# A two-tile transformer kernel: choosing the first tile's experts in lots beside the second tile's projection, with the index woven into the first

## What is computed

```python
qa, ka, va, iq, ik, iw, qb, kb, vb = split(h @ w_in)       # 2760 columns
score = einsum(relu(iq . ik), iw)                          # index: keeps the best 64 keys of each query
out_a = softmax attention of qa over the kept ka, va;  out_b = block attention of qb, kb, vb
x = x + concat(out_a, out_b) @ w_out
h = rms_norm(x)                                            # the expert layer
q = (h @ w_q).reshape(t, 8, 2, 128)                        # 8 heads, two halves
v_half, i_half = top_k(q . sub_keys, 16)                   # 128 keys a half
top_s, pos = top_k(all sums of the two halves' values, 16) # 16 experts of 16384 a head
w = softmax(top_s) * gelu(u_tab[expert] . h)
x = x + sum over 128 experts of w * v_tab[expert]
```

## Time and profile before

| what | value |
|---|---|
| median of three runs | 2173.9 us (2172.73 to 2174.57) |
| profiled execution | 2178.61 us, its span 2176.9 us |
| PE busy | 1676.0 us (77%) |
| DVE busy | 1487.9 us (68%) |
| ACT busy | 797.0 us (37%) |
| POOL busy | 649.8 us (30%) |
| moved by DMA | 747.39 MB, of it 536.90 MB by gathers; mean 343 GB/s |
| mean granted PE clock | 0.891 of full speed |

### The profile page before, as it was taken

How to read it: one execution, slowest core, us unless ns; L and a number is a source line. 1 busy time by engine, 2 the same in 40 slices (tenths; PEclk the granted TensorE clock), 3 DMA queues, 4 the chain that set the end, 5 groups by cost and what they waited for, 6 DMA issues and landing times.

```text
span 2176.9 us, 20643 instructions
## 1 busy us (share of the span) xinstructions
PE 1676.0 (77%) x6478; PEld 1014.4 (47%) x6478; DVE 1487.9 (68%) x3088; ACT 797.0 (37%) x2066; POOL 649.8 (30%) x524
## 2 busy tenths in 40 slices
PE   8688777847776865877777577665777899898998
PEld 4473333713323444332344433544333465668986
DVE  3359776798766679966666896758777464565644
ACT  1212462224324422432452234212545343444542
POOL 0003444444433443543243354435444000000000
PEclk9699988879999886999889799877889999999999
DMA  7248999999999999999999999999999775474552
GB/s 283 97 164 332 421 391 416 415 405 422 410 421 415 400 420 404 405 419 421 401 372 422 388 386 421 421 421 421 387 402 395 296 275 190 174 278 156 176 192 97
DMA packets 105947, 747.39 MB, mean 343 GB/s; under 512 B 12912, under 2 KB 13552, under 8 KB 16752
## 3 DMA queue, kind: packets, MB, share of 16 engines
q0 software_dynamic: 73728, 536.90, 60.3%
q1 hardware_dynamic: 31536, 207.08, 24.7%
q10 hardware_dynamic: 576, 2.10, 0.3%
HBM read 744.98 MB, written 1.05 MB: 343 GB/s over the span
## 4 chain that ended last, share of the span: by engine, by line
PE 41%; DMA 21%; DVE 20%; ACT 10%; issue 6%; DVEq 1%; PEldq 0%; POOL 0%; ACTq 0%; PEld 0%; SPq 0%; POOLq 0%
DMA sb_work<-in_peer_uv,sb_expert 17%; PE ps_acc L1453 11%; PE bank L492 6%; DVE sb_work L1417 5%; PE bank L1246 4%; DVE sb_x L1425 4%; PE bank L1939 2%; DMA sb_wring<-in_peer_w_q 2%; PE bank L559 2%; PE ps_acc L559 2%; ACT L1433 2%; PE ps_acc L561 2%; PE ps_acc L560 2%; PE bank L560 2%; PE bank L561 2%
## 5 line engine op out<-in xcount | busy, mean ns | idle before, releaser
L2497 POOL DMA_INDIRECT sb_work<-in_peer_uv,sb_expert x512 | 645.6, 1261 | 1033.5 <-PE ps_acc L1453 466.5
L1453 PE MATMUL ps_acc<-sb_work,sb_diag 128*128 128x512 f32 x1304 | 688.3, 675 | 314.2 <-ACT sb_diag L1442 267.9
L1417 DVE CUSTOM_DVE_ANT_0 sb_work<-sb_work,sb_h 128x1024 f32<-128x1024 f32 x512 | 619.9, 1223 | 190.4 <-DMA sb_work<-in_peer_uv,sb_expert 180.5
L1453 PEld LDWEIGHTS ps_acc<-sb_work,sb_diag 128*128 128x128 f32 x1304 | 264.7, 215 | 680.9 <-issue 672.0
L1433 ACT ACTIVATE sb_dots<-sb_dots 128x1 f32<-128x1 f32 x512 | 102.2, 200 | 527.6 <-DVE sb_dots L1417 492.6
L1425 DVE SCALAR_TENSOR_TENSOR sb_x<-sb_work,sb_weight,sb_x 128x1024 f32<-128x1024 f32 x186 | 238.5, 1282 | 81.1 <-ACT sb_weight L1434 81.1
L553 DVE TENSOR_TENSOR sb_work_r<-sb_wring,sb_work_r 128x2048 fp32r<-128x2048 f32 (+1 forms) x76 | 138.2, 1840 | 121.4 <-ACT sb_work_r L546 121.4
L546 ACT CAST sb_work_r<-sb_wring 128x2048 fp32r<-128x2048 f32 (+1 forms) x76 | 115.3, 1546 | 115.9 <-PE ps_acc L561 44.1
L1434 ACT ACTIVATE sb_weight<-sb_dots,sb_share 128x1 f32<-128x1 f32 x512 | 150.8, 294 | 16.6
L1246 PE MATMUL bank<-sb_hT,sb_wring 128*128 128x128 f32 x1024 | 125.8, 288 | 21.4 <-DMA sb_wring<-in_peer_w_q 19.3
L1246 PEld LDWEIGHTS bank<-sb_hT,sb_wring 128*128 128x128 f32 x1024 | 123.9, 204 | 24.8 <-issue 23.7
(11 more groups left out here) (326 smaller groups left out, 2154.3 us busy)
## 6 DMA issues: line engine op xcount, KB each, us to landing
sb_wring<-in_w_mix SPq DMA_DIRECT2D x36, 1024.0 KB
sb_wring<-in_peer_w_q SPq DMA_DIRECT2D x32, 1024.0 KB
sb_wring<-in_w_gate SPq DMA_DIRECT2D x32, 1024.0 KB
sb_wring<-in_w_up SPq DMA_DIRECT2D x16, 1024.0 KB
sb_wring<-in_w_down SPq DMA_DIRECT2D x16, 1024.0 KB
sb_wring<-in_mla_w_uq SPq DMA_DIRECT2D x12, 768.0 KB
sb_work<-in_hyb_w_in SPq DMA_DIRECT2D x8, 1024.0 KB, 15.0
sb_wring<-in_hyb_w_out SPq DMA_DIRECT2D x8, 1024.0 KB
```

What stands on the lines that cost most here:

```text
L1417: e.tensor_tensor_reduce(u, u, h[:, t, :], 1.0, 0.0, ALU.mult, ALU.add, dots[:, i:i + 1]).then_inc(dot_ready, 1)
L1453: last = e.matmul(ps_acc[:, b * 512:(b + 1) * 512], diag[:, number % DIAGS, :], ring[:, n % RING, D + b * 512:D + (b + 1) * 512], start=k ...
L2497: pool.indirect_dma_start(ring[:, n % RING, :], None, a["peer_uv"], bass.IndirectOffsetOnAxis(ap=expert[:, t, n % P:n % P + 1], axis=0)).t ...
```

## The change

- **First projection.** The blocks of the input projection come in the order 1, 2, 0, 3, 4, 5, in both tiles. In tile 0 the turn of the rotated heads and the index are woven into the projection's stage (`first_projection`), at fixed places between PE's half blocks; relu has two buffers.
- **open_experts** replaces `route(0, 0)` with `enter_hybrid`. The first 512 query columns and their scores come first, then tile 1's projection; the other three blocks of queries stand behind its blocks 3, 4 and 5 in the order. DVE chooses experts in four lots of two heads, each with its own `experts_ready` and its own shares. The first feed is opened at the beginning of this stage, with six points "early" (3.5 each, adds on DVE) behind lot 0 and 18 points (0.85 each, adds on PE) in each of the lots 1 to 3. ACT waits for a lot's shares before its first pick.
- The turned h of tile 1 is scaled by DVE in two instructions instead of by ACT in eight.
- **Keys** have a tile of their own, 8 KB a partition, and are loaded once a layer; SP's wait for the three engines is gone for layer 0 and is one for PE in layer 1.

`top16`, `select` and the parts of the shares are moved out of `route` and otherwise unchanged; `route` calls them for all heads at once. `index_parts` is the old `index` taken apart. Core of the diff:

```diff
-        def project_parts(xT, w, chunks, cols, empty, engine, tiles, first=None, keeps=0):
+        def project_parts(xT, w, chunks, cols, empty, engine, tiles, keeps=0, order=None,
+                          planned=None, pointed=True):
 
             per, wide = blocking(chunks)
             plan = []
             block = blocks_of(w, chunks, cols, per, wide)
-            for n0 in range(0, cols, wide):
+            for i, b in enumerate(order or range(-(-cols // wide))):
+                if planned:
+                    planned(i)
+                n0 = b * wide
                 wn = min(wide, cols - n0)
                 slots = []
                 for k in range(0, chunks, per):
-                    r = n0 // wide * (chunks // per) + k // per
+                    r = i * (chunks // per) + k // per
                     slots.append((keep(r, block(k, n0), per, wn) if r < keeps else weights(block(k, n0), per, wn), k))
                 blocks = range(0, wn, 512)
...
+            def emptied(e, first, last):
+                for _, _, bn, c0, units, _ in plan:
+                    if c0 < last and first < c0 + bn:
+                        units[-1].wait_emptied(e)
...
-        def enter_hybrid():
-            norm_act, norm_dve, _, made = norm_parts(X, H, D, None, [1])
-            units = [turns.take() for _ in range(2)]
-            project_pe, project_act, _, _ = project_parts(hT, a["hyb_w_in"], DC, EVEN_COLS, empty_even, "act", [1],
-                                                            keeps=RING)
+            return pe, act, dve
...
+        def first_projection(angles):
+            spans = (QA, KA), (KA, VA), (KA, VA), (IQ, IK), (IK, IW), (IK, IW), (QB, KB), (KB, VB)
+            R_QUERIES, R_KEYS, R_IQS, R_IKS, R_QBS, R_KBS = (rotated.n + n for n in (6, 2, 3, 5, 7, 8))
+            made = (6, 1, 2, 3, 4, 5, 7, 8)
+            base = rotated.n
+            steps = rotations(0, [base + n for n in made])
+            for _ in made:
+                rotated.plan()
+            project_pe, project_act, _, emptied = project_parts(hT, a["hyb_w_in"], DC, EVEN_COLS, empty_even, "act",
+                                                                [0], RING, EVEN_ORDER)
+            blocks = [(part, turns.take()) for part in turned_heads(0)]
+            relus = [mixed[:, 1, i * 512:(i + 1) * 512].rearrange("p (a b) -> p a b", a=4) for i in range(2)]
+            score_pe, relu_act, rank_dve = index_parts(0, [two_scores.take() for _ in range(2)], relus)
...
+            def between_pe(e, i, half):
+                at = 2 * i + half
+                if at == 4:
+                    turned_pe(e, 0, R_IQS)
+                elif at == 5:
+                    turned_pe(e, 1, R_IKS)
+                elif at == 6:
+                    for _, u in blocks[0:2]:
+                        u.wait_emptied(e)
+                    score_pe(e)
+                elif at == 7:
+                    turned_pe(e, 2, R_QUERIES)
+                elif at == 10:
+                    turned_pe(e, 3, R_QBS)
...
+            def between_act(e, i):
+                if i == 1:
+                    turned_copy(e, 0)
+                elif i == 2:
+                    relu_act(e)
+                elif i == 3:
+                    turned_copy(e, 2)
+            def act(e):
+                angles["act"](e)
+                project_act(e, between_act)
+                turned_copy(e, 4)
 
             def dve(e):
-                e.wait_ge(x_landed[1], 16)
-                norm_dve(e)
...
-                    for i in range(4):
-                        c = 4 * q + i
-                        last = e.transpose(u.ap[:, i * P:(i + 1) * P], h[:, 1, c * P:(c + 1) * P], ident[:, :])
-                    last.then_inc(u.full, 1)
-                project_pe(e, units)
...
-        keys = probs[:, :, :, :].rearrange("p a b c -> p (a b c)")
-        keys_landed = Signal(sem("keys_landed"))
-        def load_keys(layer, free_from):
+        keys_landed = sem("keys_landed")
+        def load_keys(layer):
+            scored = len(stages)
 
             def load(sp):
-                for e in ("dve", "act", "pe"):
-                    sp.wait_ge(done[e], free_from)
-                sp.dma_start(keys, a["peer_keys"][layer]).then_inc(keys_landed.sem, 16)
+                if layer:
+                    sp.wait_ge(done["pe"], scored)
+                sp.dma_start(keys[:, :], a["peer_keys"][layer]).then_inc(keys_landed, 16)
             return load
...
+        def open_experts():
+            lots = [range(2 * b, 2 * b + 2) for b in range(4)]
+            routed[0, 0] = picked = [experts_ready.plan() for _ in lots]
+            lowered = [to_act.plan() for _ in lots]
+            raised = [from_act.plan() for _ in lots]
+            weighed = [shares_ready.plan() for _ in lots]
+            norm_act, norm_dve, _, made = norm_parts(X, H, D, None, [1])
+            block = blocks_of(a["peer_w_q"][0], DC, 2 * EH * P, 4, 512)
+            plan, key_units = [], []
+            def plan_queries(b):
+                slots = [(weights(block(k, b * 512), 4, 512), k) for k in (0, 4)]
+                plan.append((slots, products.take()))
+                for s, _ in slots:
+                    given_back[s] = plan[-1][1].full_at()
+                u = scores.take()
+                u.ap = ps_scores[:, :, :].rearrange("p n s -> p (n s)")[:, 0:512]
+                key_units.append(u)
+            plan_queries(0)
+            asides[SLOTS] = keys_loads.pop(0)
+            units = [turns.take() for _ in range(2)]
+            start_experts(0, 0)
+            feeds[-1]["shares"] = weighed
+            with_queries = {4: 1, 5: 2}
+            project_pe, project_act, _, _ = project_parts(
+                hT, a["hyb_w_in"], DC, EVEN_COLS, empty_even, "act", [1], RING, EVEN_ORDER,
+                lambda i: plan_queries(with_queries[i]) if i in with_queries else None, False)
+            plan_queries(3)
+            early = [point(3.5, "pe") for _ in range(6)]
+            late = []
+            for b in range(1, 4):
+                late.append([point(0.85) for _ in range(18)])
+                feeds[-1]["limits"].append((feeds[-1]["weight"], 2 * TOP * b))
+            def pe(e):
+                def queries(b, after=()):
+                    slots, u = plan[b]
+                    u.wait_free(e)
+                    for s, _ in slots:
+                        slot_wait(e, s)
+                    for j in range(4):
+                        last = route_queries(e, u, slots, 0, j)
+                        if j == 3:
+                            last.then_inc(u.full, 1)
+                        for p in after[j] if after else ():
+                            p("pe", e)
+                def score(b):
+                    plan[b][1].wait_emptied(e)
+                    key_units[b].wait_free(e)
+                    e.wait_ge(keys_landed, 16)
+                    score_keys(e, key_units[b], b)
+                def between(e, i, half):
+                    if i in (2, 3):
+                        early[2 * (i - 2) + half]("pe", e)
+                    if i == 3 and half:
+                        queries(1, [[], early[4:5], [], early[5:6]])
+                    if i in (4, 5):
+                        section = late[i - 4]
+                        if half == 0:
+                            score(i - 3)
...
+                            for p in section[0:5]:
+                                p("pe", e)
+                            queries(i - 2, [section[5 + 3 * j:8 + 3 * j] for j in range(4)])
+                            section[17]("pe", e)
+                queries(0)
+                e.wait_ge(*made)
+                for q, u in enumerate(units):
+                    u.wait_free(e)
+                    for i in range(4):
+                        c = 4 * q + i
...
+            def act(e):
+                def raise_lot(b):
+                    e.wait_ge(to_act.sem, lowered[b])
+                    raise_shares(e, 0, lots[b], raised[b])
+                def between(e, i):
+                    if i == 1:
+                        raise_lot(0)
+                    if i in (2, 3):
+                        for p in early[2 * (i - 2):2 * (i - 2) + 2]:
+                            p("act", e)
+                    if i == 3:
+                        for p in early[4:6]:
+                            p("act", e)
+                        take_queries(e, plan[1][1], 1)
+                        take_scores(e, key_units[1], 1)
+                        for p in late[0][0:5]:
+                            p("act", e)
+                    if i in (4, 5):
+                        b = i - 2
+                        for p in late[b - 2][5:18]:
+                            p("act", e)
+                        take_queries(e, plan[b][1], b)
+                        raise_lot(b - 1)
+                        if b == 2:
+                            take_scores(e, key_units[2], 2)
```

(103 more changed lines are left out.)

395 lines of the change are left out of this document (199 added, 196 removed).

## The result

| | before | after |
|---|---|---|
| median | 2173.7 us (2172.7 to 2174.6, 4 runs) | 2156.7 us (2152.7 to 2163.7, 4 runs) |
| profiled execution, its span | 2178.6, 2176.9 us | 2163.7, 2161.9 us |
| moved by DMA | 747.39 MB | 745.30 MB |
| first product of the first attention on PE | 68.50 us | 55.71 us |
| first gather, last gather | 163.3, 1683.2 us | 132.1, 1669.4 us |

The ratio is 0.9925, with a 95% interval of 0.9899 to 0.9952: 17 us faster by the medians and 15 by the profiled pair, where 21 were forecast. The time is inside the range, 4 us above the number. The profiled execution is the slowest of its four, 7 us above the median.

A forecast was written before the change was run, and what follows sets the result against it. The prediction took DMA bytes of gathered expert rows to bound the kernel, with compute close behind. Its terms, -9 - 7 - 5 = -21, took the median from 2173.9 to 2153 us, range 2140 to 2176.

The forecast's parts named there:

- Part 1: First tile's head: ranking woven into the projection, attention on PE at 59 to 60 us instead of 68.50; -9, bounds -12 and -5.
- DVE's tail: End of the first head: two rotations of eight heads, 2.2 us each, and a copy are what is late next.
- Part 2: Opening in lots with early picks: idle queue time falls from 38.5 to 31 us; -7, bounds -15 and +11.
- Is it passed on?: First feed after the opening: 26 picks fewer save queues 65 us and DVE 46, so the queues still end last.
- My 31 us of idling: Queues in the new opening: 10.5 idle from 114 us, 14.5 from 129.5, and 6 in the late parts.
- Part 3: Keys loaded twice instead of four times, 2 x 1.05 MB fewer at 408 GB/s; -5, bounds 0 and -8.
- D: Compute takes over after the opening, keys bring nothing: 2174 to 2176, half way 2167; chance 0.20.
- half-way price: Milder case of D: 2.1 us a pick, 2173.9 - 9 + 57 - 55 = 2167.
- B: Opening does not do what it says: rows chosen earlier only lie in the ring, -9 - 5 remain, 2160; chance 0.15.
- E: Lockstep of DVE, ACT and PE: a late part takes 38 us instead of 27.5, time 2184; chance 0.10.
- the three late parts: Opening's later lots, 27.5 us each on DVE with 6.1 picks; the stage ends near 250, 57 us later.
- Row and rule: Gathers beside a busy DVE: its choosing did not slow them by the earlier trace, despite the skill's port-lock rule.

The follow-up runs named there:

- run 6: Kernel before with the new head and keys kept in their own buffer (two loads), but the old opening in two half lots: 2159.4 us, ratio 0.9921.
- run 7: The changed kernel again, unaltered, measured in the same set as the later versions: 2160.0 us, ratio 0.9926.
- run 2: Changed kernel with the head as before, leaving the opening in lots and the kept keys alone: 2171.9 us, ratio 0.9991.
- run 4: Changed kernel with four key loads instead of two, each waiting for the stage in which the keys were last read: 2164.9 us, ratio 0.9947.
- run 1: Kernel before with the new head alone (new block order and first_projection); opening, feed and keys as they were: 2162.5 us, ratio 0.9949.
- run 11: Against run 6, the first feed opened inside the old opening's second half lot, 6 dots begun before the second tile's rotation: 2149.2 us, ratio 0.9875.

## Why the prediction was right, and where it was not

**Part 1, -9, measured -12.8.** The mechanism was right, the size was not. The step that failed is DVE's tail: I had DVE wait for scores until 42.5 us and rank until 53. PE made the scores at 38.66, DVE ranked from 40.12 to 49.5 and was through the last rotation near 54. My lower bound, -12, was the case of the ranking hiding whole; that is what happened, and a little more.

**Part 2, -7, measured about 0.** Runs 6 and 7 show it (2159.4 and 2160.0), and run 2 agrees. Inside the opening the steps were close: first experts at 131.6 (forecast 144 less 9), 33 gathers before 241 us (32), rotation at 239.1 (241).

The step that failed is "Is it passed on?". I counted 46 us less work for DVE and 65 less for the queues and left the queues last. (The 32 us that I called free are those of 193 to 560 us; up to 545 they are 28.6, and that changes nothing.) The rotation began 58.8 us later than with the head alone (239.1 less 180.3), near the 57 I had, while only one pick more had been taken (27 dots begun before 241 us, against 26). But from the rotation to the feed's final add it took 56.7 us less (304.5 for 361.2), not 65. The pair from one set, run 7 against run 6, says the same: 58.8 later, 58.6 less. So the sum of the queues' busy times was no bound. My reading is that the second tile's stages are a chain over three engines in order; DVE's waits fit it, which moved from rows to ACT's weights (from 241 to 540 us 3.9 us for rows and 25.5 for weights; with the head alone 31.1 and 9.9).

A count of gaps in the profiled runs, changed kernel against head alone: from 132 to 215 us the share is 0.99 for 0.72, 83 x 0.27 = 22 us won; from 97 to 132 it is 0.23 for 0.51, 10 lost, as weights no longer stream there; from 215 to 241, 2 lost; from 241 to 540 it is 0.96 for 1.00, 12 lost. So 10 us were won up to 241 us, more than the 7 forecast, and lost behind it. Sum: -2, nothing to speak of, and the first feed ends 2 us later (543.6 for 541.5). In the pair of runs 7 and 6, both with the keys kept, 23 are won, 10, 2 and 9 lost, and the feeds end level, at 539.8 and 539.7. My 31 us of idling were 25 before the first gather and 6 behind it; measured are 27 (35 x 0.77), 1 in the opening up to 215, and 14 where I had looked for none.

**Part 3, -5, measured -4.9** (run 4 against run 7), as much as the bytes alone would cost, as forecast. Run 6 against run 1 gives the same within the noise of two sets (0.9921 and 0.9949 of their own medians).

**The sum.** -12.8 - 4.9 = -17.7 stands against -17.1 by the medians. The forecast of 2153 came within 4 us in part by luck: the 4 us more on the head took back half of the 7 that the opening did not give.

**The rivals.** D named what happened: landing waits of DVE near zero and a share under 0.97 up to 540 us (3.9 us of waits and a share of 0.96 from 241 to 540; 0.97 in run 7). Its full price, a loss of 11 us in the opening, was too high; its half-way price, 2.1 us a pick, is what the runs give (56.7 us for 27 picks), a loss of 2 that cannot be told from nothing here. What D had wrong were the keys, which it put at nothing. B gave the right outcome for the opening (0) for the wrong reason: rows did not only lie in the ring, 27 of the 33 gathered before 241 us had been used, the first one 5.6 us after its gather. E did not come: the three late parts took 25.5 us each (162.5 to 239.1), near the 27.5 I had, not 38.

**By what would show it.** Right: the first gather near 135 (132.1), 32 gathers before 241, the rotation near 241, two key loads, queues at 0.9 or more from 135 up to 241. Wrong: attention at 59 to 60 (55.7), queues full beyond 241, the last dot near 534 (542.5), the last gather 20 us earlier (13.8).

**Row and rule.** The gathers beside DVE's choice took 0.93 to 0.94 us at the median before and after (L2497, L2751), and the queues were at 0.99 beside a choosing DVE. The reading of the earlier trace rows holds: the port lock that the Trainium skill describes (SBUF — State Buffer, "Who interferes with whom") kept no queue idle here, though single gathers took up to 1.85 us in the changed opening. No run isolates a DVE instruction that could hold the ports, so the rule itself is not tested.

## What to carry to other kernels

A queue that is idle in one stage is worth filling only as far as the work put there does not make the next stages start later; count the shares of the same stretches in both kernels to the point where they meet again, not the gap alone. Prefer little filling work, beside a stage that is long anyway: six picks in the old opening (run 11) gave 10 us, while 27 in a new one only paid for the four lots that made room for them. And a wait in a queue that runs ahead holds everything behind it: for a stage just ahead it cost 43 us (2208.3 less 2164.9), for an older one nothing beyond the bytes of the loads.

## What the runs showed of the hardware

The queues hold 421 to 422 GB/s on one core for four slices of 54 us, the 25th to the 28th of the changed kernel's page, with POOL's indirect gathers and SP's weight loads mixed, and 2.10 MB more cost what that rate says (4.9 us). The Trainium skill (HBM Reference, "Specifications (TRN2)") puts the share of one core at about 358 GB/s when both cores of a pair stream and near 425 for one alone; the rows here agree with the second, and no run here shows the first.
